# A modulation projection with its weights as the moving operand: four chunks in four column groups of TensorE

## The chip, the cores and the metric

The kernel is one program on one core of a Trainium2 chip. The metric is the device time of that core in microseconds (us): the median of three runs of the kernel before is 2465.03 us (2462.48 to 2465.62). TensorE is called PE here, its weight load PEld, VectorE DVE, ScalarE ACT, GpSimd POOL, and the queue of SyncE, which issues the large DMAs, SP.

## The reference

Two transformer-like blocks run one after the other on 256 tokens of width 1024, all in float32. The change touches the first block alone, and in it only this part (the rest is cut):

```python
cond = jax.nn.silu(c)                                  # c: (1, 1024)
for layer in range(2):
    mod = cond @ mod_w[layer] + mod_b[layer]           # mod_w: (2, 1024, 6144)
    sh1, sc1, g1, sh2, sc2, g2 = [m[:, None, :] for m in jnp.split(mod, 6, axis=-1)]
    h = rms_norm(x, mix_norm_g[layer]) * (1 + sc1) + sh1
    mix = even_mixer(h, ...) if layer % 2 == 0 else odd_mixer(h, ...)
    x = x + g1 * mix
    h = rms_norm(x, ffn_norm_g[layer]) * (1 + sc2) + sh2
    x = x + g2 * moe(h, ...)
```

So a single vector of 1024 numbers is multiplied by two matrices of 1024 x 6144, 48 MB in all. Each result is wanted in one of two layouts: a shift or scale (v = 0, 1, 3, 4) with the channel on the partition (`modc`), a gate (v = 2, 5) as a row that stands in all 128 partitions (`gbc`).

## The kernel before

All weights come in pieces of 1 MB (128 partitions x 2048 floats) in the order of `weight_plan`, through three buffers `raw0` to `raw2`. SP issues the DMA of piece i when piece i-3 has been used. Most weights are split on the chip into a high and a low part (ACT copies the high part into one of three `pair` buffers, DVE and POOL subtract the low part), and a product is then three fast matmuls. The modulation weights are not split: PE reads them from `raw` in plain float32, and gives the buffer free itself (semaphore `used`).

The modulation is worked in 24 halves q of 512 output channels, two pieces (8 chunks of 128 rows) each. `MODS` says in which stage of the plan a half's weights come, `UPTO` to which q PE has gone at a named point: 4 at "start", 8 at "z" (after the attention scores of the even mixer), 10 at "R", 12 at "o", 14 at "x1" (after the even mixer's output projection), 16 at "m0" (in the first mixture of experts), 22 at "odd", 24 at "x3". `mods_to(point)` on PE multiplies, for each half, 4 blocks of 128 channels x 8 chunks: the weight block is the stationary operand, and one column of `condT` moves. The result is 4 columns of a bank. `mods_to` on DVE adds the bias and writes `modc` or, for a gate, `gcol`. A gate then needs a row: DVE builds a diagonal from `gcol` (`gate_diagonals`), PE multiplies it by ones (`gate_rows`), ACT copies the bank to `gbc`.

Every engine's program is written out in order by hand; nothing is moved by a scheduler. In the even mixer DVE also computes a causal convolution of 31 taps (`conv(n)` does the next n taps, four instructions each), laid in between its other duties; `conv(31)` does what is left, and the layer norm after it waits for the last tap. In the odd mixer ACT and DVE work through tanh, exp, reciprocals, a square root and a scan, at the lines where the modulation stands too.

Where the split of later pieces may start is fixed by `W.ahead`: `split_to(i)` or `act_split(.., i)` issues all splits that fit into the buffers before piece i is used, three pieces at the output projections.

## Time and profile before

| | |
|---|---|
| median of three runs | 2465.03 us |
| the profiled execution, its own time | 2457.28 us |
| its span from the first to the last instruction | 2455.5 us |
| mean granted clock of TensorE | 0.902 |
| PE busy | 2242.3 us, 91% |
| PEld busy | 1979.0 us |
| DVE / ACT / POOL busy | 1274.5 / 1098.5 / 1118.2 us |
| HBM read | 452.25 MB, 185 GB/s over the span |
| records of the modulation products | 1536, PE busy 309.1 us, PEld 309.5 us |

The profile has one record for each pass of a matmul: a plain float32 product stands as two MATMUL and two LDWEIGHTS records, so the 768 products are 1536. "Idle before" of a group is the time that the engine waited just before it. The clock is given as a share of full speed: 1.0 is 2.4 GHz, 0.5 is 1.2 GHz.

### The profile page before, as it was taken

How to read it: one execution, taken by the hardware profiler on the slowest of the kernel's cores; microseconds unless marked ns; L12 is line 12 of the kernel's file. 1: busy time of each engine (PE TensorE's matmuls, PEld its weight loads, DVE VectorE, ACT ScalarE, POOL GpSimd, SP SyncE). 2: the span in 40 equal slices, each digit the busy share in tenths (PEclk: the TensorE clock that was granted, in tenths of full speed). 3: DMA queues.
4: the chain of work that ended last, by engine and by line, in shares of the span. 5: the costliest groups of instructions: out<-in, count | busy, mean ns of one | idle time of the engine just before them, and what ended most of it. 6: DMA issues, size and time to landing. Idle time of an engine off the chain costs nothing.

```text
span 2455.5 us, 30359 instructions
## 1 busy us (share of the span) xinstructions
PE 2242.3 (91%) x12581; PEld 1979.0 (81%) x12581; DVE 1274.5 (52%) x1485; ACT 1098.5 (45%) x1104; POOL 1118.2 (46%) x466
## 2 busy tenths in 40 slices
PE   6899778999997897899999889999899999998998
PEld 6889667777776897777777789977799899877997
DVE  0461423665666633366666655556555545564554
ACT  0330122666665422266666544454444444454443
POOL 0300102787886301177887645442354445432453
PEclk9975666999999956699999999998999999997999
DMA  4534423887887344188888845552355555532553
GB/s 163 185 103 148 143 69 106 278 283 260 290 275 257 121 132 142 69 272 277 274 290 275 274 147 197 189 167 86 121 180 198 189 172 201 178 132 70 188 190 127
DMA packets 208441, 455.38 MB, mean 185 GB/s; under 512 B 8720, under 2 KB 20648, under 8 KB 208296
## 3 DMA queue, kind: packets, MB, share of 16 engines
q1 hardware_dynamic: 203904, 448.89, 54.5%
q10 hardware_dynamic: 4392, 4.44, 0.5%
q8 instruction: 105, 1.72, 0.3%
q14 instruction: 40, 0.33, 0.0%
HBM read 452.25 MB, written 1.05 MB: 185 GB/s over the span
## 4 chain that ended last, share of the span: by engine, by line
PE 75%; DVE 10%; ACT 7%; DMA 3%; issue 2%; POOL 2%; ACTq 0%; DVEq 0%; POOLq 0%; SPq 0%
PE bank L272 73%; DMA raw<-in_ex_w 3%; ACT pair1h L548 2%; ACT pair0h L548 2%; DVE pair1l L563 2%; PE bank L1696 2%; DVE arena L1062 1%; DVE pair0l L563 1%; DVE arena L1070 1%; ACT pair2h L548 1%; DVE catTl L1062 1%; POOL pair2l L555 1%; DVE catTl L1070 1%; DVE xres L1070 0%; POOL pair1l L555 0%
## 5 line engine op out<-in xcount | busy, mean ns | idle before, releaser
L555 POOL TENSOR_TENSOR pair1l<-raw,pair1h 128x512 fp32r<-128x512 f32 x126 | 360.0, 2857 | 372.7 <-ACT pair1h L548 372.7
L555 POOL TENSOR_TENSOR pair2l<-raw,pair2h 128x512 fp32r<-128x512 f32 x126 | 345.7, 2744 | 339.2 <-ACT pair2h L548 339.1
L555 POOL TENSOR_TENSOR pair0l<-raw,pair0h 128x512 fp32r<-128x512 f32 x127 | 346.5, 2728 | 324.0 <-ACT pair0h L548 324.0
L563 DVE TENSOR_TENSOR pair1l<-raw,pair1h 128x1536 fp32r<-128x1536 f32 x126 | 234.3, 1859 | 232.3 <-ACT pair1h L548 231.9
L548 ACT ACTIVATE pair0h<-raw 128x2048 fp32r<-128x2048 f32 x127 | 243.2, 1915 | 245.0 <-PE bank L272 163.9
L563 DVE TENSOR_TENSOR pair0l<-raw,pair0h 128x1536 fp32r<-128x1536 f32 x127 | 232.5, 1830 | 214.9 <-ACT pair0h L548 214.4
L563 DVE TENSOR_TENSOR pair2l<-raw,pair2h 128x1536 fp32r<-128x1536 f32 x126 | 230.7, 1831 | 213.4 <-ACT pair2h L548 213.1
L548 ACT ACTIVATE pair2h<-raw 128x2048 fp32r<-128x2048 f32 x126 | 241.3, 1915 | 220.2 <-PE bank L272 131.1
L548 ACT ACTIVATE pair1h<-raw 128x2048 fp32r<-128x2048 f32 x126 | 241.1, 1913 | 185.8 <-PE bank L272 127.7
L272 PEld LDWEIGHTS bank<-condT,raw 128*128 128x128 f32 x1536 | 309.5, 316 | 2.1 <-DVE catTl L1062 1.7
L272 PE MATMUL bank<-condT,raw 128*128 128x1 f32 x1536 | 309.1, 339 | 1.4 <-DVE catTl L1062 1.4
L272 PE MATMUL bank<-hTh,pair0h 128*128 128x256 f32 x592 | 166.2, 281 | 14.6 <-DVE hTl L1062 8.2
L272 PE MATMUL bank<-hTl,pair0h 128*128 128x256 f32 x592 | 165.6, 280 | 0.0
L272 PE MATMUL bank<-hTh,pair0l 128*128 128x256 f32 x592 | 165.4, 279 | 0.0
L272 PE MATMUL bank<-hTh,pair2h 128*128 128x256 f32 x512 | 143.6, 281 | 10.2 <-issue 4.4
L272 PE MATMUL bank<-hTl,pair2h 128*128 128x256 f32 x512 | 143.0, 279 | 0.0
L272 PE MATMUL bank<-hTh,pair2l 128*128 128x256 f32 x512 | 143.0, 279 | 0.0
L272 PE MATMUL bank<-hTh,pair1h 128*128 128x256 f32 x496 | 137.4, 277 | 3.5 <-DVE arena L1062 3.1
L272 PE MATMUL bank<-hTl,pair1h 128*128 128x256 f32 x496 | 137.0, 276 | 0.0
L272 PE MATMUL bank<-hTh,pair1l 128*128 128x256 f32 x496 | 137.0, 276 | 0.0
L272 PEld LDWEIGHTS bank<-hTh,pair0h 128*128 128x128 f32 x592 | 113.2, 191 | 16.7 <-issue 10.3
L272 PEld LDWEIGHTS bank<-hTh,pair0l 128*128 128x128 f32 x592 | 113.3, 191 | 0.0
(280 smaller groups left out, 5129.5 us busy)
## 6 DMA issues: line engine op xcount, KB each, us to landing
raw<-in_ex_w SPq DMA_DIRECT2D x192, 1024.0 KB, 5.2
raw<-in_mod_w SPq DMA_DIRECT2D x48, 1024.0 KB, 5.1
raw<-in_ffn_w_gate SPq DMA_DIRECT2D x44, 1024.0 KB, 5.0
raw<-in_ffn_w_up SPq DMA_DIRECT2D x44, 1024.0 KB, 5.1
raw<-in_ffn_w_down SPq DMA_DIRECT2D x44, 1024.0 KB, 5.0
raw<-in_w_in SPq DMA_DIRECT2D x20, 1024.0 KB, 5.1
raw<-in_ev_in_w SPq DMA_DIRECT2D x10, 1024.0 KB, 5.3
raw<-in_od_in_w SPq DMA_DIRECT2D x8, 1024.0 KB, 5.1
```

The lines of the kernel that those rows point to most:

```text
L272: return e.matmul(o, l, r, start=start, stop=stop, skip_group_check=True)
L548: e.activation(hi, raw, ACT.Copy).then_inc(S("hi"), 1)
L555: e.tensor_tensor(lo[:, 0:cut], raw[:, 0:cut], hi[:, 0:cut].bitcast(F32), ALU.subtract).then_inc(S("lo_pool"), 1)
L563: e.tensor_tensor(lo[:, cut:], raw[:, cut:], hi[:, cut:].bitcast(F32), ALU.subtract).then_inc(S("lo"), 1)
L1062: return e.tensor_tensor(o, a, b, op)
L1070: return e.scalar_tensor_tensor(out=o, in0=a, scalar=s, in1=b, op0=op0, op1=op1)
L1696: return e.transpose(o, i, ident)
```

## The change

The product is turned round. The condition stands: `cond32` holds for each chunk a block of 128 x 32 whose first column is that chunk of the condition and whose others are zero. A weight chunk of 128 x 512 moves past it. The four chunks of a piece go to the four column groups of the array, chunk c writing partitions 32c to 32c+31 of one bank; the second piece adds to them. So a half takes 8 products where it took 32. What stands in the bank is four partial rows (and 124 rows of zeros), so a second step follows: ACT or DVE copies the bank to `mrow` (`mod_copy`), and PE sums over the partitions (`mod_sums`): for a gate with one product ones x `mrow`, which is at once the row in all partitions, otherwise with four products that have a block of `mrow` standing and one column of ones moving. DVE then adds the bias (`mod_vector`).

The bias of a gate is no column now but a row, brought by four new DMAs of 512 KB into `gbc` (`gate_bias`, on SP). The diagonals, the rows from them and ACT's copies of them are gone. The order of three halves in `MODS` and some banks change. PE's norm no longer waits for the modulation after the output projections, and sums are made one half late, before the half after the next.

```diff
-MODS = (((0, 0), (0, 1)), ((0, 3), (0, 4), (1, 0), (0, 2)), ((1, 1), (0, 5)), ((1, 3), (1, 4), (1, 2)), ((1, 5),))
+MODS = (((0, 0), (0, 1)), ((0, 2), (0, 3), (0, 4), (1, 0)), ((1, 1), (0, 5)), ((1, 2), (1, 3), (1, 4)), ((1, 5),))
...
+            def gate_bias(l, k):
+                v = 2 + 3 * k
+                e.dma_start(gbc[:, k, :], A["mod_b"][l, v * D:(v + 1) * D].partition_broadcast(128)).then_inc(S(f"gate{k}"), 16)
+
             for i, (key, is_split, k, n) in enumerate(plan):
+                if i == W.where["ev_in_w", (0,), 0, 0]:
+                    gate_bias(0, 0)
+                    gate_bias(0, 1)
+                if key[0] == "gates":
+                    e.wait_ge(S("even_x"), 4)
+                    gate_bias(1, 0)
+                    e.wait_ge(S("moe_xv"), 2)
+                    gate_bias(1, 1)
...
+        def mod_copy(e, q, copy):
+            e.wait_ge(S("used"), mod_used(q))
+            if q >= 2:
+                e.wait_ge(S("mod_sum"), q - 1)
+            copy(mrow[:, q % 2, :], banks[mod_bank(q)][:, :]).then_inc(S("mod_row"), 1)
+
+        def mod_vector(e, own, q):
+            l, v, half = MOD_HALVES[q]
+            b = banks[sum_bank(q)]
+            e.wait_ge(S("mod_sum"), q + 1)
+            if q in GATES:
+                o = gbc[:, v // 5, half * 512:(half + 1) * 512]
+                e.wait_ge(S(f"gate{v // 5}"), 16 * (l + 1))
+                e.tensor_tensor(o, b[:, :], o, ALU.add).then_inc(S("mod"), 1)
+                return
...
-                conv(9)
+                conv(4)
+                for q in range(4, UPTO["z"]):
+                    mod_copy(e, q, e.tensor_copy)
+                    conv(1)
+                    if q > 4:
+                        mod_vector(e, own, q - 1)
...
                     e.activation(tn[:, h4, :], rr[:, h4, :], ACT.Tanh, scale=-1.0).then_inc(S("odd_tanh"), 1)
+                mod_copy(e, 16, copy)
+                mod_copy(e, 17, copy)
                 for i, h4 in enumerate(halves):
                     e.activation(rr[:, h4, :], rr[:, h4, :], ACT.Exp).then_inc(S("odd_a"), 1)
+                mod_copy(e, 18, copy)
+                mod_copy(e, 19, copy)
...
+            def mod_sums(n):
+
+                for q in range(summed[0], n):
+                    b, row = banks[sum_bank(q)], mrow[:, q % 2, :]
+                    e.wait_ge(S("mod_row"), q + 1)
+                    if q in GATES:
+                        ins = mm(e, b[:, :], ones, row, True, True)
+                    else:
+                        for f in range(4):
+                            ins = mm(e, b[:, f:f + 1], row[:, f * 128:(f + 1) * 128], ones[:, 0:1], f == 0, True)
+                    ins.then_inc(S("mod_sum"), 1)
...
                     if q >= 2:
+                        mod_sums(q - 1)
                         e.wait_ge(S("mod"), q - 1)
                     for r, i, k, views in pieces("mod_w", (l,), D, v * D + half * 512, 512):
-                        for f in range(4):
-                            for c in range(k):
-                                ins = mm(e, b[:, f:f + 1], views[0][:, c, f * 128:(f + 1) * 128], condT[:, r + c:r + c + 1],
-                                         r + f + c == 0, r + c == KC - 1)
+                        for c in range(k):
+                            ins = mm(e, b[32 * c:32 * c + 32, :], cond32[:, r + c, :], views[0][:, c, :], r == 0, r > 0)
                         ins.then_inc(S("used"), 1)
...
                 for nh in range(2):
                     part("ev_out_w", 0, nh, False, True)
+                e.wait_ge(S("even_x"), 2)
                 mods_to("x1")
-                norm(1, UPTO["x1"])
+                norm(1)
+                mod_sums(UPTO["x1"])
...
                 mods_to("odd")
                 e.wait_ge(*V("odd_yl0", 1))
+                mod_sums(UPTO["odd"])
                 part("od_out_w", 0, 0, True, False)
-                gate_rows(4)
-                e.wait_ge(S("gate"), 6)
+                e.wait_ge(S("mod"), UPTO["odd"])
                 part("od_out_w", 0, 1, True, False)
```

On PE, in the even mixer behind the attention scores (`arena`), the kernel before has this (the end of point "z"; `cst` with `arena` is the sum of point "R"):

```order
L272 MATMUL bank<-arena 128x128 x4
L272 MATMUL bank<-condT,raw_85 128x1 x16
L272 MATMUL bank<-condT,raw_86 128x1 x16
L272 MATMUL bank<-condT,raw_87 128x1 x16
L272 MATMUL bank<-condT,raw_85 128x1 x16
```

and the changed kernel, from the same place (`cond_60` is `cond32`):

```order
L272 MATMUL bank<-arena 128x128 x4
L272 MATMUL bank<-raw_84,cond_60 32x512 x4
L272 MATMUL bank<-raw_85,cond_60 32x512 x4
L272 MATMUL bank<-raw_86,cond_60 32x512 x4
L272 MATMUL bank<-raw_84,cond_60 32x512 x4
L272 MATMUL bank<-mrow,cst 128x512
L272 MATMUL bank<-raw_85,cond_60 32x512 x4
L272 MATMUL bank<-raw_86,cond_60 32x512 x4
```

A piece went from 16 products of one column to 4 of 512 columns, and between the halves there is now a sum that needs a copy made by another engine.

On DVE, at the same place, the convolution's 36 instructions stood in one block ahead of the six blocks of the attention (`arena<-bank,arena`), in the kernel before:

```order
L1070 SCALAR_TENSOR_TENSOR arena<-arena,cols 128x256 x36
L1070 SCALAR_TENSOR_TENSOR arena<-bank,arena 128x512
L1062 TENSOR_TENSOR arena<-arena,cst 128x2x128
```

In the changed kernel the copies of the halves 4 to 7 and their bias additions stand between them:

```order
L1121 SCALAR_TENSOR_TENSOR arena<-arena,cols 128x256 x16
L587 COPY mrow<-bank 128x512
L1121 SCALAR_TENSOR_TENSOR arena<-arena,cols 128x256 x4
L587 COPY mrow<-bank 128x512
L1121 SCALAR_TENSOR_TENSOR arena<-arena,cols 128x256 x4
L597 TENSOR_TENSOR gbc<-bank,gbc 128x512
L587 COPY mrow<-bank 128x512
L1121 SCALAR_TENSOR_TENSOR arena<-arena,cols 128x256 x4
L597 TENSOR_TENSOR gbc<-bank,gbc 128x512
L587 COPY mrow<-bank 128x512
L1121 SCALAR_TENSOR_TENSOR arena<-arena,cols 128x256 x4
L601 TENSOR_TENSOR modc<-bank,cols 128x4
```

Every copy waits until PE has used the half's second piece, so the taps behind it and the attention's blocks wait with it.

Later on DVE, at the even mixer's output projection, the new order is (its last 12 taps are the x48):

```order
L587 COPY mrow<-bank 128x512
L574 TENSOR_TENSOR pair1l<-raw_85,pair1h 128x1536
L574 TENSOR_TENSOR pair2l<-raw_86,pair2h 128x1536
L574 TENSOR_TENSOR pair0l<-raw_84,pair0h 128x1536
L587 COPY mrow<-bank 128x512
L574 TENSOR_TENSOR pair1l<-raw_85,pair1h 128x1536
L1121 SCALAR_TENSOR_TENSOR arena<-arena,cols 128x256 x48
```

where the kernel before had the same four splits and then 40 instructions of the convolution.

## Rows read from the trace of the kernel before

**Rows 1.** The page: the chain's shares, the modulation products as PE's group.
```profile
PE 75%; DVE 10%; ACT 7%; DMA 3%; issue 2%; POOL 2%; ACTq 0%; DVEq 0%; POOLq 0%; SPq 0%
...
...
L272 PE MATMUL bank<-condT,raw 128*128 128x1 f32 x1536 | 309.1, 339 | 1.4 <-DVE catTl L1062 1.4
```

**Rows 2.** Instructions on `condT` by stretch: busy us of PE, PEld, DVE; clock, DMA.
```profile
156.00:210.50 54.50, 54.50 (x256) 54.50 (x256) 0.00 (x0) 0.50 0.41 135
340.20:344.60 4.40, 4.40 (x41) 4.40 (x41) 0.00 (x0) 1.00 0.00 0
345.00:363.00 18.00, 18.00 (x86) 18.00 (x86) 0.00 (x0) 0.50 0.53 174
820.00:970.00 150.00, 78.23 (x384) 78.25 (x384) 0.00 (x0) 0.67 0.43 143
```

**Rows 3.** Timeline of PE: start, us, group, idle before and its releaser.
```profile
24.80 54.61 PE L272 MATMUL bank<-condT,raw 128*128 128x1 f32 x256
...
148.04 8.00 PE L272 MATMUL bank<-arena 64*128 64x256 f32 x32 [1.28 <-ACT arena L734]
155.97 9.33 PE L272 MATMUL bank<-condT,raw 128*128 128x1 f32 x43
...
242.28 4.50 PE L272 MATMUL bank<-arena 128*64 128x256 f32 x32 [0.25 <-DVE modc L1062]
...
309.30 3.78 PE L272 MATMUL bank<-arena,cst 128*128 128x256 f32 x8 [12.52 <-DVE arena L1070]
...
340.12 23.20 PE L272 MATMUL bank<-condT,raw 128*128 128x1 f32 x128
...
378.29 24.20 PE L272 MATMUL bank<-condT,raw 128*128 128x1 f32 x128
```

**Rows 4.** All engines by stretch: busy of PE, PEld, DVE, ACT, POOL; clock, DMA, GB/s.
```profile
242.30:245.00 2.70, 2.70 (x18) 2.06 (x20) 2.70 (x8) 0.00 (x0) 0.00 (x0) 0.50 0.66 168
245.60:246.80 1.20, 1.18 (x14) 0.81 (x11) 0.69 (x1) 0.20 (x1) 0.00 (x0) 0.99 0.75 290
309.00:320.00 11.00, 7.56 (x16) 5.05 (x16) 1.66 (x3) 3.02 (x4) 0.00 (x0) 0.50 0.00 0
```

**Rows 5.** The same view, the start and the first mixture of experts: what DMA reaches.
```profile
4.00:12.00 8.00, 0.00 (x0) 0.00 (x0) 0.00 (x0) 0.00 (x0) 0.00 (x0) 1.00 1.04 404
1350.00:1400.00 50.00, 45.06 (x207) 36.36 (x206) 32.65 (x29) 33.19 (x27) 38.06 (x15) 0.99 0.86 296
```

**Rows 6.** The page, DMA issues: KB each, median us from issue to landing.
```profile
raw<-in_mod_w SPq DMA_DIRECT2D x48, 1024.0 KB, 5.1
```

**Rows 7.** Timeline of ACT: the copy of a gate's bank, the norm's scaling.
```profile
286.63 0.60 ACT L694 ACTIVATE gbc<-bank 128x512 f32<-128x512 f32 x1 [4.80 <-PE bank L272]
...
345.02 1.33 ACT L665 ACTIVATE arena<-xres,small 128x512 f32<-128x512 f32 x2 [1.20 <-POOL small L573]
```

**Rows 8.** The chain that ended last: start, us, what.
```profile
81.39 2.82 DVE pair1l L563
...
87.61 46.08 PE bank L272 x288
...
288.70 1.91 ACT pair1h L548
```

**Rows 9.** Timeline of DVE: modulation, convolution and splits.
```profile
144.68 14.33 DVE L1070 SCALAR_TENSOR_TENSOR arena<-arena,cols 128x256 f32<-128x256 f32 x36
...
197.13 0.16 DVE L1062 TENSOR_TENSOR modc<-bank,cols 128x4 f32<-128x4 f32 x1 [13.49 <-PE bank L272]
...
292.31 16.94 DVE L1070 SCALAR_TENSOR_TENSOR arena<-arena,cols 128x256 f32<-128x256 f32 x40
...
880.79 3.35 DVE L1458 RECIPROCAL arena<-arena 128x512 f32<-128x512 f32 x1
```

**Rows 10.** Timeline of PE, the odd mixer's output projection, first matmul of its second part.
```profile
967.24 0.50 PE L272 MATMUL bank<-pair0h,catTh 128*128 128x512 f32 x1 [0.69 <-ACT gbc L694]
```

**Rows 11.** Timeline of SP: the gate matrices of the odd mixer are issued.
```profile
827.21 0.37 SPq L508 DMA_DIRECT2D raw<-in_od_rg_w  x1
```

More of the change, by code:

```diff
@@ L327, in program @@
         identr = sb("identr", 128, dt=F32R)
-        condT = sb("condT", KC)
         modc = sb("modc", 2, 4, KC)
@@ L564, in dve_split, with mod_used @@
                                     ).then_inc(S("lo"), 1)
+        def mod_used(q):
+            l, v, half = MOD_HALVES[q]
+            return W.last("mod_w", (l,), v * D + half * 512) + 1
+        def mod_copy(e, q, copy):
[4 more added lines that the diff above has]
+        def mod_vector(e, own, q):
+            l, v, half = MOD_HALVES[q]
+            b = banks[sum_bank(q)]
[5 more added lines that the diff above has]
+                return
+            h4 = slice(4 * half, 4 * half + 4)
+            o = modc[:, l, {0: 0, 1: 1, 3: 2, 4: 3}[v], h4]
+            ins = e.tensor_tensor(o, b[:, 0:4], c_modb[:, l, v, h4], ALU.add)
+            if v in (1, 4):
+                own.did(ins)
+                own.see()
+                own.did(e.tensor_scalar(o, o, 1.0, None, ALU.add))
+                own.see()
+                ins = e.tensor_tensor(o, o, (c_mix if v == 1 else c_ffn)[:, l, h4], ALU.mult)
+            ins.then_inc(S("mod"), 1)
         def pool_program(e):
@@ L658, in x_rms, with copy @@
                 ins.then_inc(S("x_sq"), 1)
+            def copy(o, i):
+                return e.activation(o, i, ACT.Copy)
             def norm_x(j):
@@ L687, in turn @@
                 x_rms(4 + t)
-            def gate_rows(g0):
-                for g in (g0, g0 + 1):
-                    l, v, half = MOD_HALVES[GATES[g]]
-                    e.wait_ge(S("gate_row"), g + 1)
-                    e.activation(gbc[:, v // 5, half * 512:(half + 1) * 512], banks[row_bank(g)][:, :], ACT.Copy
-                                 ).then_inc(S("gate"), 1)
             def start():
@@ L712, in start @@
                 e.dma_start(cst[:, 273:], A["constants"][:, 273:]).then_inc(S("bc"), 16)
+                for q in range(UPTO["start"]):
+                    mod_copy(e, q, copy)
                 act_split(e, ahead, W.last("mod_w", (0,), D + 512))
@@ L786, in even @@
                 norm_x(1)
+                mod_copy(e, 12, copy)
+                mod_copy(e, 13, copy)
                 norm_h(1, False)
@@ L795, in moe @@
                     e.activation(htok[0][:, th, cs], banks[4 + i][:, :], ACT.Copy).then_inc(S("tok_hi"), 1)
+                if l == 0:
+                    mod_copy(e, 14, copy)
+                    mod_copy(e, 15, copy)
                 e.wait_ge(S("gates"), l + 1)
@@ L923, in odd @@
                 norm_x(3)
+                mod_copy(e, 22, copy)
+                mod_copy(e, 23, copy)
                 norm_h(3, False)
@@ L1107, in turn, with residual @@
                 x_rms(4 + t)
[L1109 to L1138 removed]
+            def residual(stage, name, r, gate, mods):
                 for nh in range(2):
@@ L1142, in residual @@
                     e.wait_ge(S("used"), at + 1)
-                    e.wait_ge(S("gate"), gates)
+                    e.wait_ge(S("mod"), mods)
                     for th in range(2):
@@ L1159, in start @@
                 e.wait_ge(*V("cols", 4))
-                mods_to("start")
+                for q in range(UPTO["start"]):
+                    mod_vector(e, own, q)
                 split_to(W.last("mod_w", (0,), D + 512))
@@ L1256, in even @@
                 tt(eu, eu, bc(sq[:, 0:T], 4), ALU.mult).then_inc(S("even_un"), 1)
+                mod_vector(e, own, 10)
+                mod_vector(e, own, 11)
                 e.wait_ge(*V("even_uh", 1))
                 tt(catT[1][:, 0:4, :], eu, catT[0][:, 0:4, :].bitcast(F32), ALU.subtract).then_inc(S("even_ul"), 1)
-                residual("even", "ev_out_w", 0, gbc[:, 0, :], 2)
+                residual("even", "ev_out_w", 0, gbc[:, 0, :], 6)
                 norm_x(1)
-                mods_to("x1")
                 norm_h(1, False)
+                mod_vector(e, own, 12)
+                mod_vector(e, own, 13)
             def moe(l):
@@ L1344, in down @@
                             ).then_inc(S("yg_lo"), 1)
-                gate_diagonals(2 + 4 * l)
                 gathered(0, 0, (2, 3))
                 gathered(0, 1, (0, 1))
+                for q in range(14 + 8 * l, 16 + 8 * l):
+                    mod_vector(e, own, q)
                 for ex in range(NE):
@@ L1458, in odd @@
                         own.did(e.reciprocal(xb8[:, r, :], xb8[:, r, :]))
+                        mod_vector(e, own, 16 + 2 * i + r.start // 2 % 2) if i == 0 else None
                     own.see()
                     tt(tn[:, h4, :], tn[:, h4, :], xb8[:, h4, :], ALU.mult).then_inc(S("odd_m2"), 1)
-                mods_to("odd")
-                gate_diagonals(4)
+                mod_vector(e, own, 18)
+                mod_vector(e, own, 19)
                 for i, h4 in enumerate(halves):
@@ L1474, in odd @@
                     split_to(out(0, i))
-                residual("odd", "od_out_w", 512, gbc[:, 0, :], 6)
+                    mod_vector(e, own, 20 + i)
+                residual("odd", "od_out_w", 512, gbc[:, 0, :], 18)
                 norm_x(3)
-                mods_to("x3")
                 norm_h(3, False)
@@ L1789, in start @@
                 mods_to("start")
+                mod_sums(UPTO["start"])
             def even():
```

110 lines of the change are left out of this document (44 added, 66 removed).

## The prediction

> **What bounds the kernel now.** I read the page's chain of waits first: PE holds 75% of it, and among PE's groups the modulation products are the largest, 1536 records with 309.1 us busy [rows 1]. They sit on the chain: DVE, which adds the bias, stood idle 13.49 us for one half [rows 9]. Next the stretches on `condT` with the granted clock. At clock 0.50, 86 records start in 18.00 us, 0.21 us each; at 1.00, 41 in 4.40 us, 0.107 us each [rows 2]. So a half (64 records) costs 13.6 us at 1.2 GHz and 6.9 us at 2.4 GHz, and in most of its stretches these products stand at the lower level. PE and PEld are both busy without a gap there: what is paid is the load of 128 x 128 weights for one column. In the first stage 256 records take 54.61 us [rows 3], 0.213 us each: the pace of 1.2 GHz.
>
> Then DMA: while they run, the core takes 135 to 174 GB/s [rows 2], against 404 GB/s at the program's start [rows 5]. A piece of 1 MB at 404 GB/s is 2.6 us, and alone it lands 5.1 us after issue [rows 6]. With three buffers a piece every 2.6 us is possible, a half in 5.2 us. So PE, not memory, is the limit in these stages, by a factor above two.
>
> **The new product.** The trace has no 32-column product, but two neighbours. First the pace of moving columns in float32: 8 records of 256 columns in 3.78 us [rows 3] at clock 0.50 [rows 4], some 0.35 of it the last one's tail: 0.43 us each. One of 512 columns is 0.86 us, and a piece has 4 products, 8 records: 6.9 us one after the other at 1.2 GHz, 3.45 at 2.4.
>
> Second, whether column groups run side by side. The attention outputs at 242.28 are 8 products of 256 and 8 of 128 columns with 64-column weights, alternating between the two halves of the array. One after the other that is 16 x 0.43 + 16 x 0.215 = 10.3 us at 1.2 GHz, 5.2 at 2.4. They took 4.50 us [rows 3], at 0.50 until about 245.6 and at 0.99 after it [rows 4]: 3.3 / 10.3 + 1.2 / 5.2 = 0.55 of the time that the work takes in series. Two groups ran 1.8 times as fast as one. I take four groups as near four times: 1.75 us a piece at 1.2 GHz, 0.9 at 2.4. Bounds: 6.9 (no overlap, low clock) and 0.9. For the clock I count the low level, since PE will wait between pieces.
>
> The Trainium skill, "TensorE: Matmul & The Clock Gate", section on packing small matmuls, measured 2.38 times for three column tiles; that efficiency for four gives 3.2 times, an estimate of 2.2 us a piece at 1.2 GHz, and the sum below would lose about 0.45 x 48 = 21 us of its gain. The trace's 1.8 of 2 is better than that. "TensorEngine Tiling (Array Packing)", section on tiling modes, says that a change of tiling mode drains the engine, which speaks against this change with two switches a half. The trace shows the switch from the scores' 64-row tiles to full ones at 155.97, while 148.04 + 8.00 is 156.04 [rows 3]: no gap. If each of 48 switches cost one record's mean 0.34 us [rows 1], it would be 16 us.
>
> **The added steps of a half.** One bank copied, 0.60 us on ACT as for a gate before [rows 7]; the sum: 8 records of a loaded block and one column, 8 x 0.21 = 1.7 us, or for a gate two records of 512 columns, 2 x 0.86 = 1.7 us; the bias and the hops, about 0.5 us during which PE waits. The copy lies beside the next half's pieces. So a half takes PE 2 x 1.75 + 2.2 = 5.7 us in place of 13.6, and DMA's 5.2 us just keeps up. 8 of the 24 halves are gates; their old diagonals, rows and copies go.
>
> **Stage by stage**, on the times of before.
> - Start. Products began at 24.80 and took 54.61 [rows 3]. Three pieces are there; the fourth can land 5.1 us after the first is used. With 1.75 a piece and sums before the third and fourth half the last piece is used at 44.5 in place of 79.4. But now the next weights are late: after the last piece come 1 MB of gate biases (2.6 us) and two pieces, landed at about 47.7 and 50.3; split by ACT (1.91) [rows 8] and DVE (1.8) at 54. From the end of that split to the first projection it was 87.61 - 84.21 = 3.4 [rows 8]: 57.4, not 87.61. Gain 30.
> - Even mixer. From 156 on PE does halves 4 to 7 by about 177 and their sums by 180; before, until 210.5 [rows 2]. DVE has placed four copies between the taps and so reaches the attention's blocks, 7 us of work, only at 179; these were hidden under PE before and now are not. Sums of "R" end at 192, halves 8 and 9 at 200, the attention outputs at 205, halves 10 and 11, with two sums ahead, at 217. Output projection: its first piece is in at 218, split at 223, used at 231 (24 products, 8 us at a mixed clock); the fourth is split by ACT only then, as before at 288.70 [rows 8], and by DVE until 234.6. What ends last is again the convolution: 48 instructions of it are left, at 16.94 / 40 [rows 9] 20 us, to 254, against 309.30 [rows 3]. Gain 55. What is late next are these 12 taps: they were 10 before, 3.2 us less.
> - After the even mixer. PE's parts end at 340.12, then 23.20 us of products [rows 3]. Now three pieces are in the buffers and the fourth lands 5.1 us after the first is used: 8.7 us, to 348.8. The norm's input is ready at 345.02 + 1.33 [rows 7], so this is no new wait. Gain 14.
> - First experts: 24.20 us at 378.29 [rows 3] become 8.7; the routing mask, which it covered, is ready at 380. Gain 15.5, and 0.7 for ACT's two gate copies that stood ahead of the first split.
> - Odd mixer, 12 pieces, 78.23 us [rows 2]. PE runs halves 16 to 19 by 886, but half 20 waits for the bias of 18, which stands on DVE behind four reciprocals of 3.35 us [rows 9] and is made at 893. The last piece is used at 902. Then weights: ACT splits three pieces, the third landed at 908, before it can write the scan's output; DVE follows at 912, PE adds two sums (3.4) and the first part until 924. The second part waits for the last bias, behind DVE's scan and a split: 927.6 against 967.24 [rows 10]. Gain 39.6: the wait on data of ACT and DVE is the next bound here.
> - After it: as in the even mixer, 25 us of products to 8.9. Gain 16. Second experts 0.7.
>
> Sum: 30 + 55 + 14 + 16.2 + 39.6 + 16.7 = 171.5, say 172. SP's new wait for the end of the first experts' residual costs nothing: the odd mixer's norm needs that residual too, and the piece behind the wait is issued only at 827.21 [rows 11], in the middle of the odd projections. The experts after it, and the second block, stay as they are. The profiled execution's own time is 2457.28, so 2285; it lies 7.7 below the median of three runs, from which the same gain gives 2293. I predict 2288, between the two.
>
> **Rivals.**
> - Overlap or transport is worse: the column groups run one after the other but at 2.4 GHz (3.45 a piece, 8.3 a half), or DMA gives only the 296 GB/s that it gave in the experts [rows 5], 3.5 us a piece. The first costs 2.6 us x 24 = 62 (2350), the second 1.9 us for some 15 halves' pieces not in the buffers beforehand, 28 (2316). For it: float32 with four groups is nowhere in the trace. Against: 1.8 of 2, and 404 GB/s.
> - The clock rises. Columns move now; a burst of them brought it to 0.99 within 3.3 us at 242.28 [rows 4]. Then 0.9 a piece and sums of half the price; DMA's 5.2 us a half binds, 0.5 less for each, and the matmuls just behind the stages run faster by 2 to 3 us in seven places: 2288 - 12 - 18 = 2258.
> - Slower: no overlap and the clock stays low, because a quarter of the array does not raise it. A half is 2 x 6.9 + 2.2 = 16.0 us, 2.4 above 13.6; over 24 halves 58, and no gain elsewhere: 2515. It decides from 5.7 us a piece on (13.6 less 2.2, halved). Against it: 64-column weights both overlapped and raised the clock.
> - The change doesn't do what it says: PE does its products sooner but ACT, DVE and the weights' splits, which it covered, end last everywhere. That is half true in my stages already (start, convolution, odd mixer); fully true it leaves half the gain, 2370.
>
> **Chances.** Forecast 2262 to 2312: 0.62. Clock up, below 2262: 0.12. Worse overlap or transport, 2312 to 2350: 0.16. Covered work, above 2350 but faster: 0.06. Slower: 0.03; within 0.2%, about 5 us, which is what a measurement of this kernel tells from no change: 0.01. Faster by more: 0.96. Range 2248 to 2345, which leaves under 2 in 10 outside.
>
> **What would show it.** The new products' rate: 8 records a piece in 1.75 us with starts four abreast, not 6.9. DMA near 350 GB/s in the modulation's stretches. DVE's tap blocks with a copy between, the convolution's last block of 48 ending near 254 less the start's 30, about 224. In the odd mixer PE idle before half 20 for DVE. The expert and feed-forward stages must be as long as before; if they change, my sum is wrong however well it fits. It is also wrong if PE waits for copies in every half rather than for weights.

## The result and the profile after

| | median us | lowest to highest | ratio to before (95%) |
|---|---|---|---|
| before | 2463.76 | 2460.87 to 2465.62 | |
| changed | 2318.35 | 2316.21 to 2320.34 | 0.9411 [0.9394, 0.9427] |

The change saves 145.4 us, 5.9%. The forecast was 2288, with a range of 2248 to 2345: right in sign and range, 30 us too hopeful. In the profiled executions the spans are 2455.5 and 2318.5: 137.0 us, where the sum said 172. (Further down, one of ten executions of `e11_all_moved_896` took 5287.5 us and stands in no ratio.)

The page of the changed kernel. The chain's shares, then the group that stands for the 1536 records of [rows 1], then the issue rows that answer to [rows 6]:

```profile
PE 70%; DVE 11%; ACT 7%; DMA 6%; issue 3%; POOL 2%; ACTq 0%; DVEq 0%; POOLq 0%; SPq 0%
...
raw<-in_mod_w SPq DMA_DIRECT2D x48, 1024.0 KB, 6.5
```

```profile
L272 PE MATMUL bank<-raw,cond 128*32 128x512 f32 x384 | 61.3, 759 | 40.8 <-DMA raw<-in_mod_w 33.2 <-DVE gbc L597 3.9 <-DVE modc L601 3.6
```

309.1 us of products have become 61.3, ahead of which PE idles 40.8, 33.2 of them for the weights. PE fell on the chain from 75% to 70%, DMA rose from 3% to 6%: a part of the wait for the array turned into waits for transport.

The timeline of PE in the changed kernel (start, us, group, idle before and its releaser), at the start, in the even and in the odd mixer, answers to [rows 3, 10]:

```profile
25.37 3.35 PE L272 MATMUL bank<-raw,cond 128*32 128x512 f32 x24
33.16 1.77 PE L272 MATMUL bank<-raw,cond 128*32 128x512 f32 x8 [4.45 <-DMA raw<-in_mod_w]
34.86 1.87 PE L272 MATMUL bank<-cst,mrow 128*128 128x1 f32 x8
...
61.34 0.55 PE L272 MATMUL bank<-hTh,pair0h 128*128 128x256 f32 x1 [11.82 <-DVE hTl L1113]
...
123.81 8.26 PE L272 MATMUL bank<-arena 64*128 64x256 f32 x32 [1.28 <-ACT arena L775]
132.00 4.64 PE L272 MATMUL bank<-raw,cond 128*32 128x512 f32 x24
139.24 1.94 PE L272 MATMUL bank<-raw,cond 128*32 128x512 f32 x8 [2.60 <-DMA raw<-in_mod_w]
141.10 1.86 PE L272 MATMUL bank<-mrow,cst 128*128 128x512 f32 x2
...
228.23 3.53 PE L272 MATMUL bank<-arena,cst 128*128 128x256 f32 x8 [16.62 <-DVE arena L1121]
...
756.49 2.78 PE L272 MATMUL bank<-raw,cond 128*32 128x512 f32 x24
...
781.89 3.64 PE L272 MATMUL bank<-raw,cond 128*32 128x512 f32 x16 [2.81 <-DVE modc L601]
...
820.28 0.80 PE L272 MATMUL bank<-pair0h,catTh 128*128 128x512 f32 x1 [5.20 <-DVE modc L607]
```

Here is to be seen: a piece (8 records) takes 1.94 us at the low clock and 2.78 / 3 = 0.93 at the high one; the convolution's last taps still end last in the even mixer (16.62 us of PE's idle time); and the odd mixer's second part starts at 820.28, not 967.24. By the starts of single records the four chunks do run abreast: four start within 20 ns, and the next four 430 ns later at the high clock, 853 at the low one.

The switch between kinds of tiles needs the same care. The scores' 64-row tiles end at 123.81 + 8.26 = 132.07 and the new tiles start at 132.00, which looks like no gap, but ends of matmuls are modelled, and only starts are measured. The last products of the odd projections and the first modulation product, first in the kernel before (full tiles on both sides), then in the changed one (full tiles, then 32 columns), both at the high clock:

```profile
866.12 0.28 PE L272 MATMUL bank<-catTh,pair1l 128*128 128x256 f32 x1
866.24 3.96 PE L272 MATMUL bank<-condT,raw 128*128 128x1 f32 x35
```

```profile
756.17 0.28 PE L272 MATMUL bank<-catTl,pair1h 128*128 128x256 f32 x1
756.28 0.28 PE L272 MATMUL bank<-catTh,pair1l 128*128 128x256 f32 x1
756.49 0.64 PE L272 MATMUL bank<-raw,cond 128*32 128x512 f32 x4
```

The starts are 0.12 us apart without a switch and 0.21 with one. Wherever two kinds of tiles follow each other without idle time, in both kernels, the start comes 0.09 us later than it would within one kind at the high clock, and 0.13 to 0.14 at the low one (0.35 instead of 0.21 at 132.00 here, and at 155.97 in the kernel before). The changed kernel has some 20 such places more than the kernel before, up to the end of the odd mixer: 2 to 3 us, an estimate.

The timeline of DVE, as in [rows 9], and of ACT:

```profile
135.71 0.69 DVE L587 COPY mrow<-bank 128x512 f32<-128x512 f32 x1 [8.93 <-PE bank L272]
...
208.06 20.12 DVE L1121 SCALAR_TENSOR_TENSOR arena<-arena,cols 128x256 f32<-128x256 f32 x48
...
802.31 1.45 DVE L1113 TENSOR_TENSOR catTl<-arena,catTh 128x1024 fp32r<-128x1024 f32 x1 [9.92 <-ACT catTh L968]
```

```profile
799.42 1.91 ACT L559 ACTIVATE pair1h<-raw 128x2048 fp32r<-128x2048 f32 x1 [0.66 <-DMA raw<-in_od_out_w]
801.24 1.04 ACT L968 ACTIVATE catTh<-arena 128x1024 fp32r<-128x1024 f32 x1
```

DVE stands idle 8.93 us ahead of a copy, with taps queued behind it that wait for nothing but their turn, and later does 48 of them in 20.12 us while PE waits; ACT ends its splits before it writes what DVE stands for. And the chain that ended last, at the start, beside [rows 8]:

```profile
42.88 11.30 DMA raw<-in_ev_in_w
61.34 53.63 PE bank L272 x312
```

Two stretches of modulation in the view of all engines (stretch, length, busy of PE, PEld, DVE, ACT, POOL, then clock, DMA share, GB/s):

```profile
132.00:190.00 58.00, 41.50 (x217) 16.89 (x216) 33.48 (x77) 12.30 (x19) 0.00 (x0) 0.79 0.70 247
756.00:790.00 34.00, 22.68 (x117) 7.40 (x120) 25.60 (x22) 12.83 (x17) 0.00 (x0) 0.72 0.84 289
```

The clock is neither low nor high but both in turn, and memory gives 247 to 289 GB/s, up from 135 to 174 [rows 2].

Where the gain arose and where a part of it was lost, by the starts of the same instructions in both traces:

| mark | before | changed | gain so far | by the prediction |
|---|---|---|---|---|
| first projection | 87.61 | 61.34 | 26.3 | 30 |
| convolution's sums | 309.30 | 228.23 | 81.1 | 85 |
| first experts' first product | 431.51 | 315.60 | 115.9 | 115.2 |
| odd mixer, products start | 866.2 | 756.5 | 109.8 | 115.2 |
| odd mixer, second part | 967.24 | 820.28 | 147.0 | 154.8 |
| second block's first transposes | 1417.34 | 1256.06 | 161.3 | 171.5 |
| end | 2455.5 | 2318.5 | 137.0 | 171.5 |

The last line is the finding: 24.3 us of the gain are lost in the second block, which has no modulation and whose instructions the change doesn't touch. Another 6.1 are lost between the first experts and the odd mixer. The view by stretch, inside the feed-forwards' long runs of 256-column products (PE's busy time and records, clock, DMA share, GB/s), first of before:

```profile
1482.00:1502.00 20.00, 20.00 (x179) 1.00 0.76 263
```

and of the changed kernel:

```profile
1358.00:1378.00 20.00, 20.00 (x173) 1.00 0.73 257
```

The same products, PE full, clock 1.00 in both, and 3% fewer of them in 20 us. By the starts, a run of 192 takes 21.7 us before and 22.5 after: 113.4 ns each, or 117.8. Products of 512 columns there went from 229.1 to 233.3. Both kinds lose some 4 ns a product, whatever its length, so it is not the pace of the columns, and with it not the clock, that fell. Some 4 ns on each of about 6000 products in the second block is the 24 us. The two explanations that I had: the change shifted tiles in SBUF (`cond32`, 1024 bytes, replaced `gcol` and `condT`, and every tile from `rows` on moved; the split weights by 896 bytes), or the 32-column tiles leave the engine in a slower state.

### The profile page after: what moved, and what is told of

Its sections match the earlier page's. It is cut to its first block, busy times and chain, and to the rows that moved or that the text cites. A ratio compares the mean times of both kernels' runs of the same rounds, so it can differ in the third digit from the quotient of the medians.

```text
span 2318.5 us, 28344 instructions
## 1 busy us (share of the span) xinstructions
PE 2046.8 (88%) x11557; PEld 1721.7 (74%) x11557; DVE 1272.7 (55%) x1470; ACT 1101.1 (47%) x1112; POOL 1120.2 (48%) x466
## 4 chain that ended last, share of the span: by engine, by line
PE 70%; DVE 11%; ACT 7%; DMA 6%; issue 3%; POOL 2%; ACTq 0%; DVEq 0%; POOLq 0%; SPq 0%
PE bank L272 69%; DMA raw<-in_ex_w 3%; ACT pair1h L559 2%; DMA raw<-in_mod_w 2%; DVE arena L1113 2%; ACT pair0h L559 2%; DVE arena L1121 2%; DVE pair1l L574 2%; PE bank L1733 1%; DVE pair0l L574 1%; ACT pair2h L559 1%; DVE catTl L1113 1%; POOL pair1l L566 1%; POOL pair2l L566 1%; DVE catTl L1121 1%
## 5 line engine op out<-in xcount | busy, mean ns | idle before, releaser
L574 DVE TENSOR_TENSOR pair1l<-raw,pair1h 128x1536 fp32r<-128x1536 f32 x126 | 232.3, 1844 | 233.3 <-ACT pair1h L559 232.9
L574 DVE TENSOR_TENSOR pair0l<-raw,pair0h 128x1536 fp32r<-128x1536 f32 x127 | 233.3, 1837 | 227.4 <-ACT pair0h L559 227.2
L272 PEld LDWEIGHTS bank<-hTl,pair0h 128*128 128x128 f32 x592 | 114.3, 193 | 0.4
L272 PEld LDWEIGHTS bank<-hTh,pair2h 128*128 128x128 f32 x512 | 98.9, 193 | 10.7 <-issue 7.4
```

Of the source, the lines that this page charges most:

```text
L272: return e.matmul(o, l, r, start=start, stop=stop, skip_group_check=True)
L574: e.tensor_tensor(lo[:, cut:], raw[:, cut:], hi[:, cut:].bitcast(F32), ALU.subtract).then_inc(S("lo"), 1)
```

## Experiments

Times of kernels that ran on different chips are compared by their ratio to before, measured beside them. "Second block" is the span less the start of its first transposes (1038.1 before, 1062.4 changed).

**1. Old program, shifted tiles** (`e1_pad`).

```
         gbc = sb("gbc", 2, D)
+        sb("pad", 224)
```

> The kernel before, with one unused tile of 896 bytes a partition put where the changed kernel's tiles shifted: every tile from rows on stands 896 bytes higher, nothing else differs. Theory A (addresses): in the changed kernel the matmuls of the experts and feed-forwards run slower only because their operands stand at other addresses in SBUF. Then a group of 256 columns here takes 117.5 ns a matmul at full clock and not 113.3, the four feed-forwards take 6 to 7 us more each, and the whole is about 25 us slower: 2489 us. Rival B (the 32-column tiles, or something else of the new products, leave the engine slower): 113.3 ns and 2464 us, no change.

Measured: 2480.48, ratio 1.0068 [1.0043, 1.0092], 17 us slower. Second block 1066.0. The group in [rows 1]'s view went from 281 to 285 ns, and its long runs have the slow pace:

```profile
L272 PE MATMUL bank<-hTh,pair0h 128*128 128x256 f32 x592 | 168.9, 285 | 14.3 <-DVE hTl L1063 8.2
```

```profile
1481.00:1501.00 20.00, 20.00 (x172) 1.00 0.75 257
```

So 896 unused bytes, without any new product, bring the slow pace. Rival B has no part in these 28 us of the second block. Between the profiled executions the difference is 25.5 (2481.0 and 2455.5), as forecast; between the medians it is 17 to 18, less than the 25 forecast, for the profiled execution of the kernel before was one with hardly any slow products, as the table under 5 to 10 shows.

The same program gives a check of the clock in the first stage. The products on `condT`, first in the trace of the kernel before, then in that of `e1_pad` (stretch, length, busy of PE and PEld, DVE, clock, DMA share, GB/s):

```profile
30.00:80.00 50.00, 49.41 (x232) 49.32 (x232) 0.00 (x0) 1.00 0.45 147
```

```profile
30.00:80.00 50.00, 46.61 (x219) 46.52 (x219) 0.00 (x0) 0.50 0.48 160
```

Both have 0.213 us a record, which is the pace at 0.50 in [rows 2]. So a change of the clock is missing from the rows of the kernel before, and its mean of 0.902 is somewhat too high.

**2. New program, old addresses** (`e2_old_addresses`).

```
-        cond32 = sb("cond32", KC, 32)
+        sb("pad0", 16)
...
         identr = sb("identr", 128, dt=F32R)
+        sb("pad1", 16)
...
+        cond32 = sb("cond32", KC, 32)      # behind the last tile
```

> The changed kernel with the new weights' tile at the end of SBUF and two unused tiles in its place, so that every other tile stands at the address that it had in the kernel before. Theory A (addresses): the pace goes back from 117.6 to 113.3 ns for 256 columns, the feed-forwards to their old length, the whole 25 us faster than the changed kernel: 2293 us. Rival B (the new products themselves slow what follows): still 117.6 ns, 2318 us.

Measured: 2294.8, ratio 0.9314 [0.9291, 0.9337]; 23.5 us faster than the changed kernel, against 25 forecast. But the pace did not simply go back. Second block 1050.0, and there two neighbouring runs have one pace each:

```profile
1315.00:1335.00 20.00, 20.00 (x173) 1.00 0.75 262
1348.00:1368.00 20.00, 20.00 (x179) 1.00 0.77 259
```

There are two paces, with next to nothing between them; the engine changes from one to the other behind a single longer record (123 ns at 1280 us) or behind another kind of product, then keeps one for a whole run or many. With the shifted addresses 95 to 98% of the products have the slow one; with the old ones a share that differs between kernels. Theory A was right about the cause and wrong in thinking the address sets the pace outright: it sets the odds. And since the new products stand in this kernel too, and half of what follows has the fast pace, this run speaks against rival B as well.

**3. One column group in place of four** (`e3_one_column_group`). The sums take 32 partitions.

```
-   ins = mm(e, b[32 * c:32 * c + 32, :], cond32[:, r + c, :], views[0][:, c, :], r == 0, r > 0)
+   ins = mm(e, b[0:32, :], cond32[:, r + c, :], views[0][:, c, :], r + c == 0, r + c == KC - 1)
```

> The changed kernel with all eight chunks of a piece in the first column group, summed over 32 partitions only: the same number of products, none side by side. If the four column groups overlap as I predicted, the eight records of a piece now take 6.9 us at 1.2 GHz or 3.4 to 3.7 at 2.4 (0.43 or 0.22 each for a pair of passes of 256, doubled), in place of 1.9 or 1.05; where transport sets the piece at 2.6 us only the part above it counts: between 0.9 x 48 = 43 us (high clock throughout) and some 4 x 48 = 190 (low clock), and I expect 2318 + 60 = 2380, since a busier array raises the clock. Rival: transport and not PE sets these stages, then the time stays within 10 us of 2318.

Measured: 2372.18, ratio 0.9635 [0.9608, 0.9661]: 54 us slower than the changed kernel, 8 short of the forecast 2380. The same products on PE in the even and the odd mixer:

```profile
134.28 13.92 PE L272 MATMUL bank<-raw,cond 128*32 128x512 f32 x32
...
808.70 7.05 PE L272 MATMUL bank<-raw,cond 128*32 128x512 f32 x16 [0.78 <-DVE gbc L597]
```

```profile
792.00:845.00 53.00, 47.14 (x125) 13.47 (x123) 28.10 (x24) 15.54 (x20) 0.00 (x0) 1.00 0.69 221
```

Eight records take 3.5 us at the high clock (granted 1.00 in the second stretch), against 0.93 with four groups: four groups run 3.8 times as fast as one, or 4.0 times by the starts (429 ns a record against 430 for four). Here PE is busy 47.1 of 53 us, nearly all with 32-column products, and the granted clock is 1.00; in the changed kernel it is busy 22.7 of 34 at 0.72 and 41.5 of 58 at 0.79. That its waiting lowers the clock fits these rows, but no run changed the waiting alone. The second block is 1061.8, as in the changed kernel, so the use of four groups at once does not matter there; the products still have 32 columns, so rival B is not tested by this run.

**4. Less transport** (`e4_half_bytes`). A modulation piece has four chunks, not eight as my expectation says, so this kernel leaves out half of the modulation's weights, not three quarters.

```
+                if key[0] == "mod_w":
+                    k = 2
...
-   ... cond32[:, r + c, :], views[0][:, c, :], r == 0, r > 0)
+   ... cond32[:, r + c, :], views[0][:, c % 2, :], r == 0, r > 0)
```

> The changed kernel loading only the first two of a modulation piece's eight chunks' groups as its DMA (2 of 8 chunks a transfer) and using them in turn for all eight: it leaves out three quarters of the modulation's weights, all products, copies and sums stay. If waits for these pieces set the pace of the changed kernel's modulation stages (17.4 us of PE's waits between 120 and 300 us, and transport of 2.6 us a piece elsewhere), it gains 20 to 35 us: about 2290. Rival: PE's order and DVE's copies bind, transport is hidden: within 5 us of 2318.

Measured: 2298.12, ratio 0.9335 [0.9311, 0.9359]: 20 us faster than the changed kernel (19 by the ratios). By the starts, 6 are gained by the first projection, 17 by the end of the even mixer (its following products start at 241.53, not 258.18), 22 by the odd mixer, 25 by the second block. So transport is on the path at the start and in the even mixer, hardly in the odd one. Even here, with 512 KB in a median of 4.2 us, PE waits for weights:

```profile
L272 PE MATMUL bank<-raw,cond 128*32 128x512 f32 x384 | 56.0, 706 | 33.5 <-DMA raw<-in_mod_w 19.5 <-DVE modc L603 7.8 <-DVE gbc L599 6.2
```

**5 to 10. Which address, and relative to what.** The rows that differ are only the place and size of an unused tile: ahead of `rows` in the kernel before with 1024, 384 and 768 bytes (`e5_pad_1024`, `e10_pad_384`, `e12_pad_768`); ahead of `rows` in the changed one with 128 more (`e6_after_plus_128`); there ahead of the six split tiles alone (`e9_pairs_plus_128`); and in the kernel before 896 bytes ahead of `xres`, so that activations and split weights move together (`e11_all_moved_896`). The last as a diff, the others are alike:

```
+        sb("pad", 224)
         xres = sb("xres", 2, D)
```

> The kernel before with an unused tile of 1024 bytes in place of the 896 of the earlier run, all else equal. Theory A1 (what matters is how the operands' addresses stand within 1024 bytes, which this shift leaves as they were): the pace of 256 columns goes back to 113.3 ns and the time to 2462, no change from the kernel before. Theory A2 (the shift matters relative to the tiles that did not move, the activations): about 118 ns and 2480, as with 896 bytes.

> The changed kernel with one more unused tile of 128 bytes, so that its weights and its large tiles stand 1024 bytes above those of the kernel before instead of 896. Theory A1 (place within 1024 bytes): as with the old addresses, some 2295 us. A2 (distance to the unmoved tiles): 2318, no change. If the pace is one of two that the engine falls into, and addresses only weigh on which, it can come out anywhere between, with both 113 and 118 ns in its stages.

> The changed kernel with 128 unused bytes put ahead of the six tiles of split weights alone: these stand 1024 bytes above their old addresses (256 past a multiple of 1024, as before), all other tiles 896 above, as in the changed kernel. If it is the split weights' place within 1024 bytes that decides between the paces of 113 and 118 ns: about 2293 us, the second block (from its first transposes to the end) 1040 to 1050 us in place of 1062. If it is another tile's (activations in the arena, raw pieces): 2318 and 1062.

> The kernel before with an unused tile of 384 bytes: the split weights stand 640 bytes past a multiple of 1024, where they stood at 256 (fast) and, with 896 bytes, at 128 (slow). If only some places are bad, and 640 is none: 2462 us, as before, second block 1038 to 1050. If any place but the first is bad: 2480 and 1066. I have no rule that tells which, and hold both for equally likely.

> The kernel before with the unused 896 bytes ahead of xres, so that the activations (xres, hT, catT) move with the split weights and their distance stays. If the split weights' own place within 1024 bytes decides (128 here, as in the first padded kernel): 118 ns, second block 1060 to 1066 us, about 2478 us. If the distance between split weights and activations decides: 113 ns, 1038 to 1048, about 2459.

> The kernel before with an unused tile of 768 bytes: the split weights stand exactly on a multiple of 1024 bytes, the place that a round allocation would give. Bad places so far are 128 and 640, the good one 256. If only 256 (or distances equal to it) is good: 2478 us, second block 1060 to 1066. If some other places are good too and a multiple of 1024 is one: 2459 us, 1038 to 1048.

Measured, all kernels together. "Distance" is the bytes from the first activation tile `hT` to the first split tile, as both are allocated, modulo 256; "slow" the share of 256-column products in the second block that start 116 ns or more apart, in the one profiled execution of each kernel:

| kernel | split weights moved against `hT` | distance mod 256 | second block us | slow | ratio to before |
|---|---|---|---|---|---|
| before | 0 | 64 | 1038.1 | 0.06 | 1 |
| `e11_all_moved_896` | 0 (both by 896) | 64 | 1043.9 | 0.33 | 1.0005 [0.9990, 1.0021] |
| `e12_pad_768` | 768 | 64 | 1044.2 | 0.35 | 0.9992 [0.9979, 1.0006] |
| `e5_pad_1024` | 1024 | 64 | 1047.7 | 0.55 | 1.0002 [0.9988, 1.0016] |
| `e10_pad_384` | 384 | 192 | 1059.9 | 0.98 | 1.0090 [1.0056, 1.0125] |
| `e1_pad` | 896 | 192 | 1066.0 | 0.98 | 1.0068 [1.0043, 1.0092] |
| changed | 896 | 192 | 1062.4 | 0.95 | 0.9411 [0.9394, 0.9427] |
| `e2_old_addresses` | 0 | 64 | 1050.0 | 0.45 | 0.9314 [0.9291, 0.9337] |
| `e6_after_plus_128` | 1024 | 64 | 1043.2 | 0.33 | 0.9329 [0.9308, 0.9350] |
| `e9_pairs_plus_128` | 1024, these tiles alone | 64 | 1042.6 | 0.20 | 0.9362 [0.9326, 0.9397] |

Every kernel falls on its side, and so do the other four: 0.95 and 0.98 in `e3` and `e4` (192), 0.26 and 0.18 in `e7` and `e8` (64). `e9` shows by its trace that the split weights are the tiles that matter; its time does not, since its interval reaches into that of the changed kernel. `e11` put them at the place that was slow in `e1` (128 past a multiple of 1024) and kept the time: the distance to the tiles from `xres` to `gbc` decides and not the place, and among these the activations (`hT`, `catT`) are what PE reads together with the split weights. A distance changed by 768 or 1024 is as good as unchanged, by 384 or 896 it is bad; all of these fit a period of 256 bytes. My theory of a place within 1024 bytes (A1) forecast `e5`, `e6` and `e9` rightly and fell with `e11`; that a multiple of 1024 would be bad fell with `e12`. In the good class both paces occur, in whole runs, as here in `e9_pairs_plus_128`:

```profile
1647.00:1667.00 20.00, 20.00 (x172) 1.00 0.73 254
1681.00:1701.00 20.00, 20.00 (x179) 1.00 0.77 262
```

Other distances (0 and 128 modulo 256 among them) were not tried, and why the distance matters stays open.

What it costs must be read with the spread in mind. The second block takes 1038 to 1050 us at distance 64 and 1060 to 1066 at 192. At exactly the old addresses `e2` has a slow share of 0.45 where the profiled execution of the kernel before has 0.06, the lowest of all. So of the 24.3 us lost in the second block, 12 to 20 are the distance (1062.4 against 1042.6 to 1050.0 for the same change at distance 64); the rest is that this execution of the kernel before had fewer slow products than others at the same distance. By the ratios, too, the bad distance costs the old program 17 and 22 us (`e1`, `e10`) and the new one 12 to 24 (`e9`, `e6`, `e2`).

**11, 12. Better orders** (`e7_reordered`, `e8_biases_first`), both at the old addresses. In the first: gate biases fetched behind four pieces of ev_in; taps of the convolution in DVE's gaps; ACT writes the scan's first half ahead of three splits.

```
-                if i == W.where["ev_in_w", (0,), 0, 0]:
+                if i == W.where["ev_in_w", (0,), 0, 1024]:
...
-                conv(4)                                  # ahead of half 4's copy
+                conv(9)
-                    conv(1)                              # behind each copy, halves 4 to 7
+                    conv((2, 3, 3, 0)[q - 4])
...
-                act_split(e, ahead, out(0, 0))
                 for i, h4 in enumerate(halves):
                     e.wait_ge(*V(f"odd_y{i}", 1))
                     e.activation(catT[0][:, h4, :], gy[:, h4, :], ACT.Copy).then_inc(S("odd_yh"), 1)
+                    act_split(e, ahead, out(0, 0))
```

> The changed kernel at the old addresses (2294.8 measured) with three edits of order. (1) All 31 taps of the convolution stand in DVE's gaps between the copies: DVE idled 37 us there, the 12 taps that came last take 20.1 us, and PE waited 16.7 us for them; if that wait was what ended last, the even mixer is 16 us shorter. (2) In the odd mixer ACT writes the first half of the scan's output before it splits three pieces, not after: DVE stood 9.6 us for it, PE waits 12.2 us; some 8 us. (3) The first gate biases are fetched after four of ev_in's pieces and not ahead of them: they took about 2.6 us of transport while the first projection waited; 2.6 us. Sum 26.6: 2268 us. Rival: transport of the modulation's pieces binds the even mixer anyway, and the weights of its output projection (landed at about 191 us) come no sooner; the taps' gain is then given back to the wait for weights and the time stays above 2285.

> The reordered kernel of the run before (2274 us) with one edit more: in the odd mixer DVE adds the biases of both halves 20 and 21 right after the first splits, the second no longer behind the second half's scan. PE stood 10.4 us for it before the output projection's second piece. After it PE still needs the scan's second half, which DVE writes some 10 us later: so 3 to 5 us, 2270. Rival: the time is set by that second half alone, then 2274, unchanged.

The second adds, in the odd mixer's loop on DVE:

```
                     split_to(out(0, i))
-                    mod_vector(e, own, 20 + i)
+                    for q in (20, 21) if i == 0 else ():
+                        mod_vector(e, own, q)
```

Measured: `e7_reordered` 2274.26, ratio 0.9262 [0.9236, 0.9288], by the ratios 16.5 us under `e6_after_plus_128` beside which it ran, where 26.6 were forecast. `e8_biases_first` 2268.79, ratio 0.9231 [0.9205, 0.9257]. It beats both kernels: 1.9% under the changed one (0.9231 / 0.9411 = 0.981). By the starts in the profiles, the first projection came 4 us sooner in `e7` than in `e2_old_addresses` (56.65, 60.71; 2.6 forecast). From the first product of the even mixer's modulation to that of the next group it took 114.4 us, against 127.1 and 123.5 in `e2` and `e6`: 9 to 13, not 16. Part of the rest is a wait that I made myself, here on PE in `e8_biases_first`, where the bias of a gate now stands behind 12 tap instructions (4.83 us) on DVE:

```profile
141.84 3.64 PE L272 MATMUL bank<-raw,cond 128*32 128x512 f32 x16 [4.20 <-DVE gbc L599]
...
151.64 3.32 PE L272 MATMUL bank<-raw,cond 128*32 128x512 f32 x16 [4.16 <-DVE gbc L599]
...
216.26 3.51 PE L272 MATMUL bank<-arena,cst 128*128 128x256 f32 x8 [2.41 <-ACT arena L817]
```

The 16.62 us ahead of the convolution's sums are gone. In the odd mixer, from its first product to the next group's, `e2` took 82.8 us, `e7` 79.0 and `e8` 67.5: writing the first half early gives 4 and not 8 as long as the biases come late, and the biases, forecast at 3 to 5, give 11.5. PE in `e7_reordered`:

```profile
791.87 0.79 PE L272 MATMUL bank<-pair0h,catTh 128*128 128x512 f32 x1 [10.44 <-DVE modc L609]
```

and in `e8_biases_first` the only wait there:

```profile
793.71 0.51 PE L272 MATMUL bank<-pair1h,catTh 128*128 128x512 f32 x1 [1.43 <-DVE catTl L1115]
```

By medians the two kernels differ by only 5.5 us, with intervals that overlap, so that `e8` is faster than `e7` is shown by the odd mixer's starts alone. `e7` varies more from run to run (2265 to 2280) than the changed kernel (2316 to 2320); a share of slow products that differs between executions would do that, but each kernel has only one trace.

## Why the prediction was right, and where it was wrong

- **PE's products bound these stages: right.** With one column group in four the time rises by 54 us; the rival "one after the other at 2.4 GHz" was priced at 62. The first stage at 1.2 GHz, which I took from its pace alone, is right too: `e1_pad` shows 0.50 where the trace of the kernel before has 1.00.
- **A piece in 1.75 us at 1.2 GHz and 0.9 at 2.4: right**, 1.94 and 0.93. The Trainium skill, "TensorE: Matmul & The Clock Gate", section on packing small matmuls, has 2.38 times for three column tiles; here four gave 3.8, nearer to what the 64-column products of [rows 3] promised.
- **No gap at a change of tiles: wrong, but cheap.** I took 155.97 against 156.04 for it, which is a modelled end. The Trainium skill, "TensorEngine Tiling (Array Packing)", section on tiling modes, says that a change of mode drains the engine, and by the starts this case's traces agree, with 0.09 us at the high clock and 0.13 to 0.14 at the low one, where I priced 0.34.
- **DMA keeps up with 5.2 us a half: wrong, but cheap.** I took 404 GB/s and 5.1 us from issue to landing. Pieces asked for together share the way: 6.5 us in the median, 247 to 289 GB/s over a stretch where I expected 350. PE waits 33.2 us for weights. Half the bytes give 20 us back. The stages still came out near their forecast, since products and sums took less at the higher clock: two errors of opposite sign, and that they nearly cancel is luck. The price of the transport rival was off by itself: it set 7.1 us of transport a half against DMA's 5.2, where the sum had PE's 5.7, so 1.4 us and not 1.9 for 15 halves, 2309 and not 2316.
- **Low clock: half right.** 0.79 and 0.72 in the stretches instead of 0.50. The rival "clock rises" is partly true; its gain went into waits for weights.
- **Start: 26.3 for 30.** The two first pieces of ev_in were in flight with a gate bias and a weight piece and landed 11 us after issue, at 51.5 and 54.2, not 47.7 and 50.3.
- **Even mixer: 54.8 for 55.** The named last work (12 taps, 48 instructions in 20.12 us, ending at 228.2, forecast "about 224") is what the trace shows.
- **Odd mixer: 37.2 for 39.6**, counted from its first product (866.2 and 756.5). PE waited for DVE ahead of half 20, as said, but only 2.8 us. ACT's three splits ahead of the scan's output were named, and they held DVE for 9.9 us.
- **"The experts after it, and the second block, stay as they are": wrong, the step that failed.** It holds for the instructions and not for their addresses. The term was put at nothing; the second block came out 24.3 us longer, 12 to 20 of it by the distance. Of the 10 before it some 8 are the slow pace as well, an estimate: in the first block about 2600 products of 512 columns start 233.0 ns apart instead of 230.8, and of about 960 with 256 columns nearly all are slow instead of half. At a good distance the same change gives 0.9314 to 0.9362, 2292 to 2298 us, beside the forecast 2288: the sum of the change itself was about right. The chance for 2312 to 2350 was held for another cause (transport), so the time fell into that case mostly for a reason not on my list, and that it stayed inside the range is luck.
- **What would show it.** I had written that a change in the expert and feed-forward stages would make the sum wrong however well it fits, and that is what happened. DMA near 350 GB/s was not seen either. PE idle ahead of half 20, the block of 48 near 224 and the new products' rate were, and PE waited for weights (33.2 us) far more than for biases (7.5).

## What to carry to other kernels

A tile that is added, dropped or resized moves all tiles behind it; compare the pace of untouched matmuls at the same clock, by their starts, before looking for the cause of a time in the edit, and do not size the effect from one execution of each kernel. Where a weight-stationary product bound by its load moves one column, let the weights move and put the chunks in four column groups: here that ran 3.8 times as fast as one group, and what remains is transport and the small copies between the engines. When such a stage shrinks, reorder the vector engine's filler work at once, and let no bias or copy that PE waits for stand behind it.

## What the hardware showed that I had not expected

- Float32 products over 256 columns have two paces, 113.4 and 117.8 ns (512 columns: 229.1 to 229.8 in the mean of the good kernels, 233.3 in the bad), at granted clock 1.00. Which one holds goes by whole runs of products, and its odds hang on the distance between the weights' and the activations' addresses: 64 modulo 256 gives a slow share of 0.06 to 0.55, 192 gives 0.95 to 0.98.
- Such a pace is worth 10 to 28 us in 1040 between single executions here, and 12 to 24 between medians.
- Four products in four column groups start within 20 ns and take the time of one, 430 ns over 512 columns at the high clock. A change from one kind of tile to another delays the next start by 0.09 us at the high clock and 0.13 to 0.14 at the low one, and the modelled ends in a profile hide it.
- PE busy 47.1 of 53 us on one group of 32 columns is granted 1.00; with four groups, which finish sooner and then wait, 0.72 and 0.79.
- 1 MB asked for alone lands after 5.1 us; three asked for within 3 us (134.0 to 136.7 in the changed kernel) land after 5.2, 7.5 and 9.1.
